# A gated delta rule in chunks of 128 with 32x32 inverses on GpSimd, and the layer input spilled to DRAM

## What is computed

```python
def gated_delta_chunked(q, k, v, g, beta):      # chunks of 64 in the reference
    gc = jnp.cumsum(g, axis=-1)                 # per chunk
    decay = jnp.where(incl, jnp.exp(diff), 0.0) # exp(gc_i - gc_j), i >= j
    a = jnp.where(strict, einsum(kb, k) * decay, 0.0)
    u, w = triangular_solve(a + I, [v * beta, kb * exp(gc)])
    aqk = einsum(q, k) * decay
    def step(state, inp):
        v_new = u_i - w_i @ state
        o = qd_i @ state + aqk_i @ v_new
        state = state * exp(gl_i) + kd_i.T @ v_new
# o_dn = rms_norm(o_fwd + o_bwd) * silu(z);  h = h + merged @ w_o
```

## Time and profile before

| | |
|---|---|
| time, median of 3 runs | 4578.23 us (4573.45 to 4579.26) |
| span of the profiled execution | 4567.2 us |
| delta rule (first DMA to the first DMA of the attention) | 1156 to 2482 us |
| PE busy over the whole span | 87% |
| DVE, ACT, POOL busy | 37%, 30%, 11% |

### The profile page before, as it was taken

How to read it: one execution, slowest core, us unless ns; L and a number is a source line. 1 busy time by engine, 2 the same in 40 slices (tenths; PEclk the granted TensorE clock), 3 DMA queues, 4 the chain that set the end, 5 groups by cost and what they waited for, 6 DMA issues and landing times. The chain is left out here.

```text
span 4567.2 us, 57225 instructions
## 1 busy us (share of the span) xinstructions
PE 3985.5 (87%) x22097; PEld 3437.4 (75%) x22097; DVE 1695.9 (37%) x2361; ACT 1376.0 (30%) x2387; POOL 485.9 (11%) x692
## 2 busy tenths in 40 slices
PE   6867999596799999999997878298889999999978
PEld 4656878475699999999997767186768888888757
DVE  5434000165233443333333555423333333333433
ACT  3543122152234443444442333401121111111031
POOL 0000000000334433334331000200000000000000
PEclk8888999798557776777677999699989999999989
DMA  2222122121211111111111010413101111111011
GB/s 73 71 66 63 66 88 78 47 85 67 73 39 52 48 43 52 39 52 52 39 41 50 35 57 34 162 65 123 43 23 38 37 37 32 37 37 34 29 37 60
DMA packets 294143, 251.50 MB, mean 55 GB/s; under 512 B 13387, under 2 KB 266438, under 8 KB 293862
## 3 DMA queue, kind: packets, MB, share of 16 engines
q1 hardware_dynamic: 293024, 248.75, 17.6%
q10 hardware_dynamic: 966, 0.46, 0.0%
HBM read 182.15 MB, written 67.01 MB: 55 GB/s over the span
## 5 line engine op out<-in xcount | busy, mean ns | idle before, releaser
L366 ACT ACTIVATE w_hi<-w_stage 128x1024 fp32r<-128x1024 f32 (+1 forms) x158 | 161.2, 1022 | 1062.7 <-PE psum L381 894.8
L381 PE MATMUL psum<-x_hi,w_hi 128*128 128x512 f32 (+1 forms) x1584 | 403.9, 364 | 85.2 <-DVE x_lo L300 36.2
L370 DVE TENSOR_TENSOR w_lo<-w_stage,w_hi 128x1024 fp32r<-128x1024 f32 (+1 forms) x158 | 186.5, 1182 | 772.3 <-ACT w_hi L366 770.6
L381 PE MATMUL psum<-u_hi,w_hi 128*128 128x512 f32 x1296 | 336.2, 369 | 114.5 <-DVE w_lo L370 95.8
L381 PE MATMUL psum<-x_lo,w_hi 128*128 128x512 f32 (+1 forms) x1584 | 398.7, 360 | 0.0
L381 PE MATMUL psum<-x_hi,w_lo 128*128 128x512 f32 (+1 forms) x1584 | 397.1, 359 | 0.0
L381 PEld LDWEIGHTS psum<-x_hi,w_hi 128*128 128x128 f32 x1584 | 266.4, 190 | 142.2 <-issue 69.8
L381 PEld LDWEIGHTS psum<-u_hi,w_hi 128*128 128x128 f32 x1296 | 221.5, 194 | 161.0 <-DVE w_lo L370 96.5
L381 PE MATMUL psum<-u_lo,w_hi 128*128 128x512 f32 x1296 | 329.2, 363 | 0.0
L381 PE MATMUL psum<-u_hi,w_lo 128*128 128x512 f32 x1296 | 327.2, 361 | 0.0
L1197 ACT ACTIVATE dn_u_b<-dn_tu 64x256 f32<-64x256 f32 x480 | 199.0, 415 | 421.5 <-DVE dn_tu L1143 384.4
(11 more groups left out here) (217 smaller groups left out, 6284.4 us busy)
## 6 DMA issues: line engine op xcount, KB each, us to landing
w_stage<-in_w_in_dram SPq DMA_DIRECT2D x54, 512.0 KB, 4.0
dn_rows_in<-rows_gc_beta SPq DMA_DIRECT2D x80, 256.0 KB, 3.1
w_stage<-in_w_up_dram SPq DMA_DIRECT2D x32, 512.0 KB, 4.0
w_stage<-in_w_down_dram SPq DMA_DIRECT2D x32, 512.0 KB, 3.8
gates<-gate_buf SPq DMA_DIRECT2D x16, 640.0 KB, 4.3
dn_kqT_in<-dn_qkT SPq DMA_DIRECT2D x160, 64.0 KB, 2.4
dn_v_in<-dn_v SPq DMA_DIRECT2D x80, 128.0 KB, 3.2
dn_o<-dn_ob SPq DMA_DIRECT2D x80, 128.0 KB
```

Source lines behind the costliest of these rows:

```text
L366: e.activation(self.hi[:, s, :], self.stage[:, s, :], ACT.Copy).then_inc(self.high, 1)
L370: e.tensor_tensor(self.lo[:, s, :], self.stage[:, s, :], self.hi[:, s, :].bitcast(F32), ALU.subtract).then_inc(self.split, 1)
L381: ins = e.matmul(outs[c], w(k), x(k)[:, n0:n1], start=(k == 0 and n == 0), stop=(k == n_k - 1 and n == 2))
```

## The change

A **unit** `n` (again 40) is now one tile of 128 tokens, one direction, and four of the eight heads; the chunk is the whole 128 tokens. `phase_delta` is written out as a list of 63 **slots** (-20 to 42) without a loop; in each slot every engine runs pieces of several units:

- First pass (two units in each of four slots out of eight): scores (L965), decay on DVE, POOL (L1215, L1220) and ACT, giving `at`, which stays in SBUF for 16 units, and `aq`, which SP stores to DRAM.
- Eight units are a **group** `g`. When a group's `at` is there, SP copies its 32x32 diagonal blocks to DRAM (`gather_blocks`, eight DMAs of 32x16 runs of 128 bytes), waits, and loads them as one 128x1024 tile. The group has 128 such blocks, one for each partition, and POOL inverts them side by side by substitution (`invert`, 60 dependent instructions and four more over 1024 or 32 elements, in four parts over four slots). SP stores the result twice and loads it back into block matrices (`store_inverse`, `load_inverse`, 2 x 16 DMAs).
- Level (eight slots ahead of the scan): two levels of merging, 32 to 64 (L973, L981, L983) and 64 to 128 (L990, L998), give the inverse `tt`.
- Scan: k times the state (L1009), the right side on DVE, `tt` times that (L1023), then output and new state (L1036, L1037, L1040). There is no `u` and no `w`, and one step over the state for 128 tokens.

Beside that, `phase_scalars` makes one more column of decays, `phase_load` loads into a buffer that lives for the first phases only, the first norm's SP list stores it to DRAM (5.2 MB, with a wait), and `hooks_residual` loads it back at the head of the `w_o` phase's SP list.

```diff
+    def first_pass(slot):
+        group, m = (slot + 3) // PER + 2, (slot + 3) % PER
+        n = PER * group + 2 * m
+        return [n, n + 1] if m < 4 and valid(n) else []
+    def inverse_at(slot, lag):
+        group = (slot - lag) // PER + 2
+        return group if (slot - lag) % PER == 0 and 0 <= group < GROUPS else None
+    SLOTS = range(-2 * PER - 4, NQ + 3)          # PER = 8, NQ = 40, GROUPS = 5
...
+                def gather_blocks(g):
+                    e.wait_ge(S.at_ready, PER * (g + 1))
+                    for d in range(2):
+                        for b in range(4):
...
+                    e.wait_ge(S.blk_out, 128 * (g + 1))
...
+                    e.dma_start(ga[:, :, :], d_at[g].rearrange("d b c s j -> (d b c) s j")).then_inc(S.g_landed, 16)
+                def store_inverse(g):
+                    e.wait_ge(S.inv_done, g + 1)
...
+                    e.wait_ge(S.inv_out, 32 * (g + 1))
...
+                for slot in SLOTS:               # SP
+                    for n in first_pass(slot)[:1]:
+                        load_scores(n)
+                    for n in first_pass(slot + 1):
+                        load_rows(n)
+                    for n in first_pass(slot - 1):
+                        store_aqk(n)
+                    if valid(slot - 3):
+                        store_out(slot - 3)
+                    if (slot + 3) % 2 == 0 and valid(slot + 3):
+                        load_scan((slot + 3) // 2)
+                    if (g := inverse_at(slot, 1)) is not None:
+                        gather_blocks(g)
+                    if (g := inverse_at(slot, 6)) is not None:
+                        store_inverse(g)
...
+                        load_inverse(g, 0)
+                    if (g := inverse_at(slot, 9)) is not None:
+                        load_inverse(g, 1)
...
+                for slot in SLOTS:               # PE
+                    level, first = slot + PER, first_pass(slot)
...
+                        level_x5(level)
...
+                        from_keys(slot)
...
+                        level_t5(level)
...
+                        scores(first[0])
...
+                        new_values(slot - 1)
...
+                        level_x6(level)
...
+                        output_and_state(slot - 2)
...
+                        level_tt(level)
...
+                        scores(first[1])
...
+                def invert(g, part):             # POOL
...
+                    for j in range(8 * part + (part == 0), min(8 * part + 8, 31)):
+                        m = 31 - j
+                        outer = gt[:, 0:m * j].rearrange("p (i k) -> p i k", k=j)
+                        inv.then(e.tensor_tensor(outer, gb[:, j + 1:32, j:j + 1].to_broadcast([P, m, j]),
+                                                 gb[:, j:j + 1, 0:j].to_broadcast([P, m, j]), ALU.mult))
+                        inv.then(e.tensor_tensor(gb[:, j + 1:32, 0:j], gb[:, j + 1:32, 0:j], outer, ALU.add))
...
+    def sync(self, e):                           # Norm
+        if self.copy is not None:
+            e.dma_start(self.copy.rearrange("k p t -> p k t"), self.hT[:, :, :]).then_inc(self.copied, 16)
+            e.wait_ge(self.copied, 16)
...
+        def sync_start(e):                       # hooks_residual
+            e.dma_start(hT[:, :, :], src.rearrange("k p t -> p k t")).then_inc(landed, 16)
```

More of the change, by code:

```diff
@@ L781, in _ @@
                     h0 = d * VH
[L782 removed]
+                    for kind, b in ((0, d), (3, 2 + d), (4, 6 + d)):
                         ins = e.tensor_copy(cols[:, :, kind, h0:h0 + VH], core.ps[b][:, 0:NT * VH].rearrange("p (t h) -> p t h", h=VH))
@@ new lines, in phase_delta @@
+    ends = lambda n: step_of(n) in ((NT_P - 1, NT - 1) if dir_of(n) == 0 else (NT - NT_P - 1, NT - 1))
+    with_state = lambda n: sum(not fresh(m) for m in range(n))
+    with_update = lambda n: sum(not ends(m) for m in range(n))
+    def first_pass(slot):
[5 more added lines that the diff above has]
+        return group if (slot - lag) % PER == 0 and 0 <= group < GROUPS else None
@@ L953, in _ @@
+                for z in range(2):
+                    e.wait_ge(o_stored[z], 16 * (NQ // 2))
             @block.tensor
             def _(e):
-                @if_any
-                def scores(unit):
-                    n, z = index(unit), unit[1] % 2
-                    wait_inputs(e, unit)
-                    e.wait_ge(S.kq_read, n + 1)
-                    for h in range(2):
-                        for d in range(2):
-                            ins = e.matmul(ps_kq[half(h), d, :, :], kqT[:, z, d, 0, half(h)], kqT[:, z, d, :, half(h)], start=True, stop=True)
-                    ins.then_inc(S.kq_full, 1)
@@ new lines, in _ @@
+                e.memset(dd[:, :, :, :, :], 0.0)
+                e.memset(tt[:, :, :, :, :, :], 0.0)
+                e.memset(x5[:, :, :, :], 0.0).then_inc(S.zeroed, 1)
+                for slot in SLOTS:
+                    level, first, ahead = slot + PER, first_pass(slot), first_pass(slot + 1)
+                    if valid(slot):
+                        right_sides(slot)
+                    if valid(level):
+                        level_t5(level)
+                    for n in ahead:
+                        decay_exponent(n)
+                    if (slot + 1) % 2 == 0 and valid(slot + 1):
+                        scaled_inputs((slot + 1) // 2)
+                    if first:
+                        decayed(first[0])
+                    if valid(slot - 2):
+                        new_state(slot - 2)
+                    if first:
+                        decayed(first[1])
@@ L1274, in _, with decay, decay_from_start @@
-                for sem in (S.ex_ready, S.atb_ready, S.wu_out, o_out[1]):
-                    e.sem_inc(sem, 1)
-                e.wait_ge(S.zeroed, 1)
-                run(e, turn)
+                def decay(n):
+                    e.wait_ge(S.masked, n + 1)
+                    e.activation(rf[:, n % 4, 0, :, :], rf[:, n % 4, 0, :, :], ACT.Exp).then_inc(S.e_ready, 1)
+                def decay_from_start(td):
+                    e.wait_ge(in_landed[td % 3], 80 * (td // 3) + 80)
+                    e.activation(eg[:, td % 3, :, :], eg[:, td % 3, :, :], ACT.Exp).then_inc(S.eg_ready, 1)
@@ new lines, in new_values, with output @@
+                def new_values(n):
+                    e.wait_ge(S.tr_full, n + 1)
+                    if n >= 2:
+                        e.wait_ge(S.os_full, n - 1)
+                    if not ends(n):
+                        for c in range(4):
+                            e.activation(vd[:, n % 2, c, :], ps_tr[:, c, :], ACT.Copy, scale=col(n, 3)[:, c:c + 1])
+                    e.activation(vn[:, n % 2, :, :], ps_tr, ACT.Copy).then_inc(S.vn_ev, 1)
+                def output(n):
+                    e.wait_ge(S.os_full, n + 1)
+                    if n >= 2:
+                        e.wait_ge(o_stored[n % 2], 16 * (n // 2))
+                    e.activation(ob[:, n % 2, :, :], ps_o, ACT.Copy).then_inc(S.o_ev, 1)
@@ new lines, in _ @@
+                for slot in SLOTS:
+                    level = slot + PER
+                    if valid(level):
+                        level_x5(level)
+                        level_t5t(level)
+                    if valid(slot - 1):
+                        new_values(slot - 1)
+                    if valid(level):
+                        level_x6(level)
+                    if valid(slot - 2):
+                        output(slot - 2)
+                    if valid(level):
+                        level_tt(level)
+                    for n in first_pass(slot + 1):
+                        decay(n)
+                    if (slot + 2) % 2 == 0 and valid(slot + 2):
+                        decay_from_start((slot + 2) // 2)
@@ L1317, in phase_attention @@
+                e.wait_ge(S.consts, 16)
+                for slot in SLOTS:
+                    for n in first_pass(slot + 1):
+                        mask(n)
+                    for n in first_pass(slot + 1):
+                        with_beta(n)
+                    for part in range(4):
+                        if (g := inverse_at(slot, 1 + part)) is not None:
+                            invert(g, part)
 def phase_attention(core, ct, d_q, d_k, d_v, dst):
```

704 lines of the change are left out of this document (281 added, 423 removed).

## The result

| | kernel before | changed kernel |
|---|---|---|
| time, median (range) | 4577.79 us (4573.45 to 4579.26; four runs, one more than above) | 4017.51 us (4008.71 to 4021.96) |
| ratio, 95% interval | 1 | 0.878 (0.875 to 0.881) |
| span of the profiled execution | 4567.2 us | 4011.5 us |
| delta rule, in the trace | 1326 us | 756 us (1154.45 to 1910.77) |
| moved by DMA | 251.50 MB | 317.83 MB |

The forecast was 4015 us and the measurement 4017.5, inside the range. The place is right too: the delta rule gives back 570 us, the reload of `hT` takes 13 of them again, and the span falls by 556. Inside the stage, however, the sum came out by chance: the term for the four rounds is 82 us too small, and two others together are 80 us too large.

What follows compares the result with a forecast made beforehand. PE bound the delta rule; afterwards a chain through POOL and DRAM would. Terms 52 + 404 + 246 = 702, plus 44 for the clock, gave 746 us instead of 1326; with +16 and 11 around the span, 4015 us, range 3920 to 4270.

Steps and rivals of the forecast that it cites:

- reload of `hT`: Head of the w_o phase: loading hT back delays ACT's first work on the weights, +15 us, 13 to 18.
- the term for the four rounds: Delta rule, from one group's last `at` to the next one's: four rounds of 101 us for eight slots each.
- eleven slots with scan alone, last store: End of the delta rule: 20 calls and a DVE and ACT chain, 7.7 us a slot, 85 us; store 5.
- clock, on top of all: PE in the delta rule: a quarter of 352 us at the low clock, half hidden in waits, 44 us.
- store of the spill: First norm's SP list: storing 5.2 MB takes 15 us but costs nothing, or 15 us without cover.
- The first rival: Delta rule: PE remains the bound at 1.2 GHz and its slots hide the chain, 4268 us; chance 0.17.
- The inverse: POOL's substitution for each group: 60 instructions 35.6 us, 46 us in all, plus 5 us of decay instructions inside.
- The rival of dear rows: POOL's inverse: short rows cost 0.05 us each, making it 92 us and the total 4245; chance 0.16.
- the slower case: POOL's inverse: each short row costs 168 ns, inverse 202 us, total 4750, slower than before; chance 0.06.
- The gather: SP's copy of diagonal blocks to DRAM: 8 us with issue and landing, bounds 5.5 and 15.
- One round is 55 + I: Delta rule: gather, tile load, inverse, decay, stores, loads, then 25 us of first pass add to 101 us.
- 472 + 5 I: Delta rule before the clock term: 472 us plus five times the inverse's 46 us, 702 us.

Runs made afterwards that it cites:

- e5: Changed kernel with the scan's five loads of a pair and the output's stores issued by ACT's queue instead of SP's: 4013.0 us.
- e2: Changed kernel with the scores' keys and queries in three half-size buffers, each loaded a slot ahead, instead of one buffer for a pair: 3992.4 us.
- e3: Changed kernel with the decay work of a first pass's first pair moved three slots earlier, ahead of POOL's inverse: 3964.3 us.
- e1: Changed kernel without the 60 substitution instructions of each group on POOL, so the inverses are not computed: 3925.3 us.
- e10: Changed kernel with first-pair decay work ahead of the inverse, hT's reload behind two weight loads, and dd, tt, x5 cleared later: 3942.4 us.

## Why the prediction was right, and where only the sum was

| term | predicted | measured |
|---|---|---|
| start, to the first gather | 52 | 60.5 |
| four rounds | 4 x 101 = 404 | 94.6 + 110.6 + 135.4 + 145.3 = 486 |
| last group, to its first level | 76 | 75.5 (1700.99 to 1776.48) |
| eight slots with level and scan | 80 | 82 (to 1858.36, the last level) |
| eleven slots with scan alone, last store | 90 | 52 (to 1910.77) |
| clock, on top of all | 44 | inside the above |
| stage | 746 | 756 |
| reload of `hT` | 15 | 13.4 |
| store of the spill | 0 | 0 |

**What bounds the stage** was right: PE's calls fell to 1584, and PE is no longer the bound, but idle for two fifths of it. The first rival, PE at 1.2 GHz throughout, is refuted by the mean clock of 0.76 and the 0.281 us a call; the estimate that a quarter of the calls run at the low clock was near (29%).

**The inverse** was right: 36.9 us of substitution for 35.6, and 49 to 52 us from POOL's first copy to its last with the decay work inside (47 in the last group, without), for 46 + 5. The rival of dear rows, and with it the slower case, is refuted: the shortest rows, 30 elements in all, take 0.25 us. The three instructions over 1024 elements, estimated at 2.4 us each, take 3.8, 2.8 and 1.9 us.

**The gather** took 5.9 us, issue and landing, in round 1, where the estimate was 8 and a double price for short runs would have made 15. In the second group it took 6.6 us and in the last three 9.3 to 11.7, where the five scan loads stand ahead of it (6 to 7 without them, e5). The rule of the Trainium skill that was weighed (DMA: Bandwidth & Descriptors, Specifications) is not borne out here as a double price: the gather's 5.9 us are near the lower bound of the prediction, 5.5, at which bytes alone count.

**The step that failed is "One round is 55 + I", with its last term, two slots with scores at 9 us, above all.** Round 1, in which nothing but the first pass runs, came out as worked (94.6). From the inverse's store to the next gather the traces have 36, 47, 59 and 67 us, for 38 in the sum; from the gather to the store 59, 64, 77 and 78, for 63. So of the 82 us that the rounds are over, 57 lie behind the store and 25 ahead of it. In rounds 3 and 4 all stages of the pipeline run at once, and there

- a slot of a first pass takes 18 to 25 us and not 9 (the last two of a round 22 and 18, then 25 and 24). In the two shown above, 9 are idle time, for keys that had one buffer and stood in SP's list behind other loads, and the calls behind it cost about twice, at the low clock. The sum took the slot from PE's calls at the high clock and let the load lie beside them. More buffers alone take only part of it away (e2);
- the decay work inside the inverse was costed at its own 5 us, but not for those who wait for it. The rule to name what is queued behind a wait was applied to SP and not to POOL: three of four parts of the inverse (36 us) stand ahead of a mask, ACT waits for the mask, PE for ACT, 19.8, 23.3 and 22.0 us in rounds 2 to 4. Taking the first pair's decay work ahead of the inverse is worth 53 us (e3), though most of this wait only moves to the second pair;
- so the inverse's result is not what these rounds wait for: SP came to it late, and I is worth half as much as in 472 + 5 I (e1).

**What paid for it.** The rest of the stage was 36 us shorter: eleven scan slots go through in 52 us, 4.7 each, which is the price of 20 calls at the high clock (4.45) and not the 7.7 of a chain over DVE and ACT. The clock's 44 us were added on top of terms that the measured ones contain; no run shows them as a term of their own, and what the trace shows is PE at a mean clock of 0.76 in the stage. With these 80 us the rounds' 82 were covered. The start was 8.5 us longer than in the sum, and the span came out 4011.5 us for 4003. The rest was luck of another kind: the 11 us that the prediction adds for what lies around the span are mostly the difference between one execution and the median. The record lists 1.8 us between the time and the span of a run (4013.32 and 4011.5 for the profiled one here), and the median lies 4.2 us above that run. So the total came out 2.5 us off, and it does not confirm the chain.

**What was to show it** gave the same mixed answer: POOL's two lines at 0.54 us (0.59 forecast), the stage at 756 us (745), ACT 17 us behind SP at `w_o` (19), all as said. PE's idle time before the scores, "once in eight slots for about ten us", is there in each round, behind the 16 loads of the inverse: 10.1, 8.0, 7.4 and 9.4 us. But ten more waits for keys make it 94 us, and there is as much again before L981. DVE beside POOL was costed at nothing; L1095 took up to 2.98 us instead of 1.22, as L1544 in the earlier trace rows, but no run here separates what that is worth.

## What to carry to other kernels

In a pipeline whose engines work through fixed lists, put what others wait for ahead of long work that nobody needs yet (53 us in e3); price four short instructions by what they are queued behind and who waits for them, not by their own length. A slot's price is that of its calls only if its inputs can land while the slot before still works; here, with one buffer and one list of loads, load and work took turns, and the calls behind each idle stretch cost about twice, at the low clock. When one wait is removed and nothing happens, look for the wait that took its place before giving up the edit: the half buffers on top of e3, and the second pair's early work on top of e10, each gave nothing, and together they gave the fastest kernel.

## What was not expected of the hardware

POOL and DVE slow each other in both directions. The last substitution step but one, with 58 elements, took this in round 2 without DVE's instructions on two SBUF operands beside it, and in round 4 beside them:

```profile
1366.23 0.28 POOL L1230 TENSOR_TENSOR dn_gt<-dn_gb 128x58 f32<-128x58 f32 x1
1366.59 0.29 POOL L1232 TENSOR_TENSOR dn_gb<-dn_gb,dn_gt 128x58 f32<-128x58 f32 x1
...
1617.14 0.61 POOL L1230 TENSOR_TENSOR dn_gt<-dn_gb 128x58 f32<-128x58 f32 x1
1617.83 1.16 POOL L1232 TENSOR_TENSOR dn_gb<-dn_gb,dn_gt 128x58 f32<-128x58 f32 x1
...
1617.53 1.30 DVE L1092 TENSOR_TENSOR dn_v_in<-dn_v_in,cols 128x1024 f32<-128x1024 f32 x1
1618.76 1.32 DVE L1095 TENSOR_TENSOR dn_eg<-dn_eg,dn_kq_in 128x1024 f32<-128x1024 f32 x1
```

The short instructions lose most: from 0.29 to 1.16 us, about as long as DVE's instruction of 1.30 us beside it. In the other direction, L1095 took 2.98 us beside POOL's L1225 (at 1571.45) and 1.22 alone. And POOL's copy of 1024 elements on 64 partitions with a transposing read (L1225, 3.8 us) takes twice as long as the transposing copy on 128 partitions without a factor (L1235, 1.94 us).
